# Block products in the two feed-forward layers of a 4-layer network: seven for eight

## The chip, the cores and the metric

The kernel is one program on one core of a Trainium2 chip, in float32. The metric is the device time of one execution in microseconds (us), lower is better. Time before: median 2104.29 us of 3 executions (2102.86 to 2108.72).

## The reference, cut to what matters

The network has 256 tokens of width 1024. Two layers with a mixture of 32 experts come first; then two layers of another block, each a mixer and a gated feed-forward. The change is in the feed-forwards (and in the order in which the weights of the second mixer, `mixer_c`, are loaded):

```python
def rmsnorm_2(x, g):
    xf = x.astype(jnp.float32)
    return xf * lax.rsqrt(jnp.mean(xf * xf, axis=-1, keepdims=True) + EPS) * g

def swiglu(x, w1, w3, w2):
    return (jax.nn.silu(x @ w1) * (x @ w3)) @ w2
...
        x = x + rmsnorm_2(mix, norm_g[layer, 1])
        h = rmsnorm_2(x, norm_g[layer, 2])
        x = x + rmsnorm_2(swiglu(h, ffn_w1[layer], ffn_w3[layer], ffn_w2[layer]), norm_g[layer, 3])
```

Here h is 256 x 1024, w1 and w3 are 1024 x 2816, w2 is 2816 x 1024.

## The kernel before, in words

**Stages.** The program is a list of stages. In each, TensorE (PE), VectorE (DVE), ScalarE (ACT) and GpSimd have their own instruction list; every engine waits at a stage's end until all four are through (`run_stages`, L235). SyncE (SP) runs beside them and only issues the loads of weights, in one fixed order.

**The ring.** Weights go through a ring of 6 slots of 2 MB (`WeightRing`). SP issues unit n as soon as TensorE has released the unit that held the slot before (L250, L251). A release is a drain of TensorE with an increment of `weights_used`.

**Feed-forward, up.** `feed_forward` (L1909) cuts the 2816 columns of w1 and w3 into chunks of 512 (the last one 256). A unit is one chunk of w1 or of w3. For each tile f of 128 columns (22 of them, `FT`) TensorE makes 8 matmuls with w1 and 8 with w3 (L1937): the weights' 128 x 128 block is the stationary operand, hT (h transposed: 128 channels x 256 tokens) the moving one. Both results lie in one PSUM bank. ScalarE takes the silu of the first half (L1972), VectorE multiplies it with the second half into aT (L1978). TensorE waits for a bank only from the ninth tile on. The first two tiles' products with tokens 0 to 127 are made earlier, by `up_ahead` (L1895), while the norm of tokens 128 to 255 is still being computed; `c_ahead` (L1904) does the same for the mixer behind the first feed-forward.

**Feed-forward, down.** A unit is 4 row tiles of w2 (the last one 2), 6 units in all. For each row tile and each half of the tokens TensorE makes two matmuls (L1945), with aT's 128 x 128 block as stationary and 512 columns of w2 as moving operand, into 4 banks. The last two units go first over tokens 0 to 127, then over 128 to 255, so that the first half's result is ready early.

**The norm behind it.** `residual_norm` handles the result by halves of the tokens, t = 0 and t = 1: ScalarE squares it out of PSUM (L1797), VectorE and ScalarE make the root, VectorE scales (L1824) and adds to x (L1827). Unless it is the last layer, a second norm follows on x (L1805 to L1834), TensorE turns the result (L1849), ScalarE and VectorE bring it to hT (L1811, L1838). TensorE's order: turns of t = 0, the work ahead, turns of t = 1.

**A float32 matmul in the trace** is two records of MATMUL and two of LDWEIGHTS. So L1937 has 704 matmuls and 1408 records.

Of the kernel before, what the change touches and what calls it, by code (L numbers as in the profile page):

```python
# [13 lines left out]
ALU = mybir.AluOpType  # L14
ACT = mybir.ActivationFunctionType
# [5 lines left out]
P = 128  # L21
D = 1024
S = 256
TT = S // P
KD = D // P
# [124 lines left out]
def columns(w, c0, n):  # L150

    return w[:, c0:c0 + n].rearrange("(k p) n -> p k n", p=P)


def build_program(nc, A, out):

    with ExitStack() as ctx:
# [3 lines left out]
        def sem(name):  # L161
            return ctx.enter_context(nc.semaphore(name))
# [59 lines left out]
        chain = {}  # L222
# [17 lines left out]
        def release(pe):  # L240

            pe.drain().then_inc(weights_used, 1)
# [1523 lines left out]

        def residual_norm(ready, n, scale_cols, ahead=None):

# [13 lines left out]
            halves = [slice(512 * half, 512 * half + 512) for half in range(2)]  # L1782
            each = 1 if scale_cols is None else 2

            def at(t):
# [8 lines left out]
            def act_tile(act, t):  # L1794
                act.wait_ge(ready, base + 2 * t + 2)
                for half in range(2):
                    ins = act.activation(xn[:, t, halves[half]], ps[:, 2 * half + t, :], ACT.Square,  # L1797
                                         accum_out=ssq[:, 2 * half + t:2 * half + t + 1])
# [14 lines left out]
            def dve_tile(dve, t):  # L1813
# [9 lines left out]
                for half in range(2):  # L1823
                    ins = dve.scalar_tensor_tensor(out=xn[:, t, halves[half]], in0=ps[:, 2 * half + t, :], scalar=r,  # L1824
                                                   in1=row_gain[:, halves[half]], op0=ALU.mult, op1=ALU.mult)
                v(ins)
                dve.tensor_tensor(x[:, t, :], x[:, t, :], xn[:, t, :], ALU.add).then_inc(x_ready, 1)  # L1827
                if scale_cols is None:
                    return
# [4 lines left out]
                dve.tensor_scalar(xn[:, t, :], x[:, t, :], r, None, ALU.mult).then_inc(scaled, 1)  # L1834
                for k in (0, 1, 4, 5):
# [46 lines left out]
        block_ready = sem("block_ready")  # L1882
        ffn_signals = [sem(f"ffn_{n}") for n in ("up_ready", "silu_done", "act_ready")]

# [22 lines left out]
        def feed_forward(layer, scale_cols, ahead=None):  # L1907
# [5 lines left out]
            for c, n in chunks:  # L1913
                ring.add(("w1", c), columns(w1, c, n), KD, n)
                ring.add(("w3", c), columns(w3, c, n), KD, n)
            for r, n in rows:
                ring.add(("w2", r), w2[r * P:(r + n) * P, :].rearrange("(k p) n -> p k n", p=P), n, D)
# [3 lines left out]
            silu = take(2, S)  # L1921
            up_ready, silu_done, act_ready = ffn_signals
            pe_tile, act_after, dve_after = residual_norm(block_ready, 2 * layer + 1, scale_cols, ahead)
            f0 = FT * layer

            def pe_(pe):
                f = 0
                for c, n in chunks:
                    a = ring.take(pe, ("w1", c))
                    b = ring.take(pe, ("w3", c))  # L1930
                    for j in range(n // P):
                        if f >= 8:
                            pe.wait_ge(act_ready, f0 + f - 7)
                        s0 = P if f < F_AHEAD else 0
                        for i, w in enumerate((a, b)):
                            for k in range(KD):
                                ins = pe.matmul(ps[:, NEXT_BANKS[f % 8], i * S + s0:(i + 1) * S], w[:, k, j * P:(j + 1) * P],  # L1937
                                                hT[:, k, s0:S], start=(k == 0), stop=(k == KD - 1))
                        ins.then_inc(up_ready, 1)
                        f += 1  # L1940
                    pe.drain().then_inc(weights_used, 2)
                pe.wait_ge(act_ready, f0 + FT)
                def down(w, r, k, t):
                    for half in range(2):
                        ins = pe.matmul(ps[:, 2 * half + t, :], aT[:, r + k, t * P:(t + 1) * P],  # L1945
                                        w[:, k, 512 * half:512 * half + 512], start=(r + k == 0), stop=(r + k == FT - 1))
                        if r + k == FT - 1:
                            ins.then_inc(block_ready, 1)

                for r, n in rows[:-2]:  # L1950
                    w = ring.take(pe, ("w2", r))
                    for k in range(n):
                        for t in range(TT):
                            down(w, r, k, t)
                    release(pe)
                units = [(r, n, ring.take(pe, ("w2", r))) for r, n in rows[-2:]]
                for t in range(TT):
                    for r, n, w in units:
                        for k in range(n):
                            down(w, r, k, t)  # L1960
                        if t == TT - 1:
                            release(pe)
                for t in range(TT):
                    pe_tile(pe, t)

            def act_(act):
                load_gain(act, 2 * layer + 1, A["norm_g_2"][layer, 3])
                for f in range(FT):
                    act.wait_ge(up_ready, f0 + f + 1)
                    if f >= 2:  # L1970
                        act.wait_ge(act_ready, f0 + f - 1)
                    act.activation(silu[:, f % 2, :], ps[:, NEXT_BANKS[f % 8], 0:S], ACT.Silu).then_inc(silu_done, 1)  # L1972
                act_after(act)

            def dve_(dve):
                for f in range(FT):
                    dve.wait_ge(silu_done, f0 + f + 1)
                    dve.tensor_tensor(aT[:, f, :], silu[:, f % 2, :], ps[:, NEXT_BANKS[f % 8], S:2 * S], ALU.mult).then_inc(act_ready, 1)  # L1978
                dve_after(dve)
# [479 lines left out]
        def mixer_c():  # L2459
            n0 = len(ring.units)  # L2460
            UNIT_ORDER = (2, 3, 0, 1, 4, 5, 6, 7)
            for c in UNIT_ORDER:
                ring.add(("c_in", c), columns(A["c_w_in_2"][0], 512 * c, 512), KD, 512)
            for c in range(2):
                ring.add(("c_out", c), columns(A["c_w_out_2"][0], 512 * c, 512), KD, 512)
            stream.append(stream_units(n0, len(ring.units)))
            take = carve(0, 17 * 1024)
# [395 lines left out]
```

## Time and profile before

| what | before |
|---|---|
| median time of 3 executions | 2104.29 us |
| span of the profiled execution | 2101.5 us |
| TensorE busy in the span | 1719.3 us (82%) |
| VectorE / ScalarE busy in the span | 492.5 / 233.1 us |
| feed-forward 0: up, down, norm and work ahead | 1447.9 to 1596.9, to 1674.7, to 1686.2 us |
| feed-forward 1: up, down with the final norm | 1867.0 to 2015.9, to 2101.5 us |

Of the profiled execution only the span is given; the median over the executions is 2.8 us above it. Read the table from the bottom: the two feed-forwards are 472.8 us of the span, in which the load of weights is far from its limit and TensorE is at work nearly all the time.

### The profile page before, as it was taken

How to read it: one execution, taken by the hardware profiler on the slowest of the kernel's cores; microseconds unless marked ns; L12 is line 12 of the kernel's file. 1: busy time of each engine (PE TensorE's matmuls, PEld its weight loads, DVE VectorE, ACT ScalarE, POOL GpSimd, SP SyncE). 2: the span in 40 equal slices, each digit the busy share in tenths (PEclk: the TensorE clock that was granted, in tenths of full speed). 3: DMA queues.
4: the chain of work that ended last, by engine and by line, in shares of the span. 5: the costliest groups of instructions: out<-in, count | busy, mean ns of one | idle time of the engine just before them, and what ended most of it. 6: DMA issues, size and time to landing. Idle time of an engine off the chain costs nothing.

```text
span 2101.5 us, 23283 instructions
## 1 busy us (share of the span) xinstructions
PE 1719.3 (82%) x9372; PEld 998.6 (48%) x9373; DVE 492.5 (23%) x1197; ACT 233.1 (11%) x574; POOL 92.8 (4%) x125
## 2 busy tenths in 40 slices
PE   5999978866575578776766658989999999999998
PEld 3654544322222154332222215767885486678853
DVE  1213452110111126411101104962000113320001
ACT  1002121000000011000000002322000122220000
POOL 1001001000000000840000000000000000000000
PEclk9999999987878789998787879999999999999999
DMA  9969259999999994999999996215435444124330
GB/s 361 406 249 375 111 216 396 421 421 422 422 422 422 398 405 167 413 406 421 422 422 422 422 416 250 80 64 188 159 121 194 169 148 159 42 99 151 120 140 20
DMA packets 122668, 581.16 MB, mean 277 GB/s; under 512 B 10820, under 2 KB 15272, under 8 KB 67160
## 3 DMA queue, kind: packets, MB, share of 16 engines
q1 hardware_dynamic: 120416, 573.92, 68.2%
q10 hardware_dynamic: 1064, 3.17, 0.5%
q0 software_dynamic: 1104, 2.86, 0.4%
q8 instruction: 63, 1.03, 0.2%
q14 instruction: 21, 0.17, 0.0%
HBM read 578.88 MB, written 1.05 MB: 276 GB/s over the span
## 4 chain that ended last, share of the span: by engine, by line
PE 56%; DMA 30%; DVE 6%; issue 3%; SPq 2%; ACT 1%; DVEq 1%; PEldq 0%; PEld 0%; ACTq 0%
DMA ring_buffer<-in_exp_w 29%; PE ps L1937 14%; PE ps L1945 7%; PE ps L1355 7%; PE ps L1380 4%; PE ps L2507 4%; PE ps L748 3%; PE ps L1872 3%; PE ps L506 2%; PE ps L761 1%; PE ps L910 1%; PE ps L2498 1%; SPq L1249 1%; DMA ring_buffer<-in_ada_w 1%; PE ps L859 1%
## 5 line engine op out<-in xcount | busy, mean ns | idle before, releaser
L1355 PE MATMUL ps<-ring_buffer,arena 128*32 128x512 f32 x2048 | 304.5, 752 | 183.2 <-DMA ring_buffer<-in_exp_w 180.6
L1937 PE MATMUL ps<-hT,ring_buffer 128*128 128x256 f32 (+1 forms) x1408 | 293.5, 370 | 5.2 <-issue 2.7
L1937 PEld LDWEIGHTS ps<-hT,ring_buffer 128*128 128x128 f32 x1408 | 256.5, 190 | 41.8 <-issue 6.4
L1355 PEld LDWEIGHTS ps<-ring_buffer,arena 128*32 128x32 f32 x2048 | 81.1, 134 | 393.4 <-issue 333.9
L1380 PE MATMUL ps<-ring_buffer,arena 128*32 128x512 f32 x1088 | 152.9, 714 | 93.1 <-DMA ring_buffer<-in_exp_w 82.1
L1945 PE MATMUL ps<-ring_buffer,arena 128*128 128x512 f32 x352 | 154.2, 595 | 3.0 <-DVE arena L1978 1.9
L1380 PEld LDWEIGHTS ps<-ring_buffer,arena 128*32 128x32 f32 x1088 | 40.7, 129 | 194.1 <-issue 181.4
L1551 DVE TENSOR_TENSOR arena<-arena,ps 128x512 f32<-128x512 f32 x18 | 19.1, 1063 | 415.2 <-PE ps L1355 415.2
L1945 PEld LDWEIGHTS ps<-ring_buffer,arena 128*128 128x128 f32 x352 | 65.9, 190 | 90.4 <-issue 87.8
L1978 DVE TENSOR_TENSOR arena<-arena,ps 128x256 f32<-128x256 f32 x44 | 18.5, 421 | 279.6 <-ACT arena L1972 279.6
L1324 PEld LDWEIGHTS ps<-arena,xn 128*128 128x128 f32 x640 | 73.3, 192 | 14.0 <-issue 13.9
L2507 PE MATMUL ps<-hT,ring_buffer 128*128 128x256 f32 (+1 forms) x384 | 77.7, 363 | 2.4 <-DVEq L238 1.3
L1324 PE MATMUL ps<-arena,xn 128*128 128x128 f32 x640 | 76.1, 277 | 0.7 <-DVE arena L1521 0.7
L2507 PEld LDWEIGHTS ps<-hT,ring_buffer 128*128 128x128 f32 x384 | 67.6, 190 | 12.8 <-issue 3.3
L1472 ACT ACTIVATE arena<-ps,mod,gain 128x128 f32<-128x128 f32 x72 | 27.1, 457 | 389.5 <-PE ps L1324 389.5
L748 PE MATMUL ps<-hT,ring_buffer 128*128 128x256 f32 x256 | 57.8, 387 | 4.1 <-ACTq L238 3.4
L1396 PE MATMUL ps<-arena 128*128 128x512 f32 x128 | 59.3, 605 | 0.0
L1569 DVE TENSOR_TENSOR arena<-ps,gates 128x512 f32<-128x512 f32 x16 | 11.1, 692 | 201.4 <-PE ps L1380 201.4
L1872 PE MATMUL ps<-ring_buffer,hT 128*128 128x512 f32 x128 | 56.0, 595 | 1.0 <-DVEq L238 0.8
L1489 ACT ACTIVATE arena<-ps 128x512 f32<-128x512 f32 x18 | 10.8, 597 | 409.8 <-PE ps L1355 409.8
L506 PE MATMUL ps<-ring_buffer,arena 128*32 128x512 f32 x384 | 49.6, 636 | 8.0 <-DMA ring_buffer<-in_ada_w 7.2
L748 PEld LDWEIGHTS ps<-hT,ring_buffer 128*128 128x128 f32 x256 | 49.4, 194 | 13.7 <-ACTq L238 3.5
(512 smaller groups left out, 1629.4 us busy)
## 6 DMA issues: line engine op xcount, KB each, us to landing
ring_buffer<-in_exp_w SPq DMA_DIRECT2D x384, 1024.0 KB, 18.6
ring_buffer<-in_ffn_w SPq DMA_DIRECT2D x30, 2048.0 KB, 9.1
ring_buffer<-in_ada_w SPq DMA_DIRECT2D x24, 2048.0 KB, 12.6
ring_buffer<-in_c_w_in SPq DMA_DIRECT2D x8, 2048.0 KB, 9.0
ring_buffer<-in_attn_w_in SPq DMA_DIRECT2D x6, 2048.0 KB, 17.1
ring_buffer<-in_ab_w_in SPq DMA_DIRECT2D x3, 2048.0 KB, 20.3
ring_buffer<-in_ffn_w SPq DMA_DIRECT2D x6, 1024.0 KB, 9.2
ring_buffer<-in_attn_w_o SPq DMA_DIRECT2D x2, 2048.0 KB, 12.9
```

What stands on the lines that cost most here:

```text
L506: pe.matmul(ps[g * WIDE:(g + 1) * WIDE, COND, :], spread_c[:, 2 * pair + k, row:row + WIDE], w[:, k, 512 * n:512 * (n + 1)], start=(first ...
L748: ins = pe.matmul(ps[:, n % BANKS, 0:S], w[:, k, j * P:(j + 1) * P], hT[:, k, :], start=(k == 0), stop=(k == KD - 1))
L761: ins = pe.matmul(ps[:, n % BANKS, :], hT[:, k, t * P:(t + 1) * P], w[:, k, :], start=(k == 0), stop=(k == KD - 1))
L1324: ins = pe.matmul(ps[:, BXA + k // 4, (k % 4) * P:(k % 4 + 1) * P], xn[:, t, k * P:(k + 1) * P], pick[:, t, :], start=(t == 0), stop=(t == ...
L1355: ins = pe.matmul(ps[c, bank, :], tokens[:, 4 * phase + k, c], halves[j][:, k, :], start=(phase == 0 and k == 0), stop=(phase == 1 and k = ...
L1380: ins = pe.matmul(ps[c, bank, :], tokens[:, 2 * phase + k, c], halves[j][:, k, half * 512:(half + 1) * 512], start=(phase == 0 and k == 0) ...
L1396: ins = pe.matmul(ps[:, 2 * half + t, :], weights[:, t, :], values[:, half * 512:(half + 1) * 512], start=opens, stop=False, skip_group_ch ...
L1472: return eng.activation(o, src, ACT.Identity, scale=G[:, k:k + 1], bias=H[:, k:k + 1])
L1872: ins = pe.matmul(ps[:, 2 * c + t, :], fT[:, k, t * P:(t + 1) * P], w[:, k, :], start=(k == 0), stop=(k == KD - 1))
L1937: ins = pe.matmul(ps[:, NEXT_BANKS[f % 8], i * S + s0:(i + 1) * S], w[:, k, j * P:(j + 1) * P], hT[:, k, s0:S], start=(k == 0), stop=(k == ...
L1945: ins = pe.matmul(ps[:, 2 * half + t, :], aT[:, r + k, t * P:(t + 1) * P], w[:, k, 512 * half:512 * half + 512], start=(r + k == 0), stop= ...
L2507: ins = pe.matmul(ps[:, NEXT_BANKS[n % 8], s0:S], w[:, k, j * P:(j + 1) * P], hT[:, k, s0:S], start=(k == 0), stop=(k == KD - 1))
```

## The change

In the feed-forwards most matrix products are made on 2 x 2 blocks by seven block products with sums before and after, in place of eight (Winograd's form of Strassen's method).

- **Up.** The first chunk (tiles 0 to 3, `PLAIN`) is as before. The other 18 tiles go as N = 9 pairs: a pair is two column tiles of w1 and of w3, cut in two over channels (4 + 4 tiles of 128) and over the columns; h is cut over channels and tokens. Each of the seven products is 2 x 4 matmuls (w1 and w3, four channel tiles) with 128 moving columns. VectorE makes the sums of h once (`sum_h`), three sums of the weights for each pair and one in place (`sum_w`), and joins the products (`join`). ScalarE copies four partial sums out of PSUM for each pair (`keep`) and takes one silu of 512; VectorE multiplies (`gate`).
- **Down.** The rows of w2 in a unit are cut in two, the columns in 512 + 512, the tokens in 128 + 128. VectorE sums aT (`sum_a`) and w2 (`sum_w2`); each product has half as many matmuls as the unit has row tiles, with 512 moving columns, and its own PSUM bank. The last three units go product by product. VectorE then adds the products (`dve_` and `rest_of_second`, which runs inside `dve_tile` of t = 0, behind its last scaling). The norm reads SBUF (`mixed`) where it read PSUM.
- **Ring.** The feed-forwards use slots 0 to 3; the sums lie in slots 4 and 5 (`piece`) and in spare parts of the arena. The loads of `mixer_c` get written-out slots, and all but the first wait for the end of the first feed-forward's stage.

The core of the diff:

```diff
+            UP_ORDER = (P5, P1, P2, P3, P6, P4, P7)
+            DOWN_ORDER = (P1, P2, P6, P5, P3, P7, P4)
+            LAST = 3
...
+                    pe.wait_ge(sums_done, summed("w", g))
+                    if g >= 2:
+                        pe.wait_ge(sums_done, summed("joined", g - 2))
+                    elif g == 1:
+                        pe.wait_ge(act_ready, a0 + PLAIN)
+                    for product in UP_ORDER:
+                        if product in (P3, P6, P7):
+                            pe.wait_ge(kept, kept0 + 4 * g + (P3, P6, P7).index(product) + 1)
+                        name, opens, stationary, moving = operands[product]
+                        o = region(g, name)
+                        for m in range(2):
+                            for k in range(4):
+                                ins = pe.matmul(o[:, m * P:(m + 1) * P], stationary(m, k), moving[:, k, :],
+                                                start=(opens and m == k == 0), stop=(k == 3), skip_group_check=True)
+                        ins.then_inc(part_ready, 1)
...
+                for v in range(len(rows) - LAST):
+                    w = ring.take(pe, ("w2", rows[v][0]))
+                    pe.wait_ge(sums_done, summed("a", v))
+                    pe.wait_ge(sums_done, summed("w2", v))
+                    for product in DOWN_ORDER:
+                        if v == 0 and product in (P1, P5):
+                            pe.wait_ge(sums_done, summed("joined", N - 2 + (P1, P5).index(product)))
+                        down(v, w, product)
                     release(pe)
...
+                    v(dve.tensor_tensor(s3, w11, w21, ALU.subtract))
+                    v(dve.tensor_tensor(w21, w21, w22, ALU.add))
+                    v(dve.tensor_tensor(s2, w21, w11, ALU.subtract))
+                    dve.tensor_tensor(s4, w12, s2, ALU.subtract).then_inc(sums_done, 1)
...
+                sum_h()
+                sum_w(0)
+                for f in range(2):
+                    gate_plain(f)
+                sum_w(1)
+                for f in range(2, PLAIN):
+                    gate_plain(f)
+                dve.wait_ge(act_ready, a0 + PLAIN)
+                sum_a(0)
+                for g in range(N):
+                    join(g)
+                    if g + 2 < N:
+                        sum_w(g + 2)
+                    if g == N - 2:
+                        sum_w2(0)
+                    gate(g)
+                    if g % 2 or g == N - 1:
+                        sum_a(1 + g // 2)
+                for i in range(1, len(rows)):
+                    sum_w2(i)
...
+            def rest_of_second(dve):
+                v = chain["dve"]
+                dve.wait_ge(part_ready, down_part(P7))
+                v(dve.tensor_tensor(first_sum, first_sum, ps[:, DOWN_BANK[P7], :], ALU.add))
+                dve.tensor_tensor(mixed(1, 1), second_sum, ps[:, DOWN_BANK[P7], :], ALU.add).then_inc(block_ready, 1)
+                dve.wait_ge(part_ready, down_part(P4))
+                dve.tensor_tensor(mixed(1, 0), first_sum, ps[:, DOWN_BANK[P4], :], ALU.add).then_inc(block_ready, 1)
...
-            for c in UNIT_ORDER:
-                ring.add(("c_in", c), columns(A["c_w_in_2"][0], 512 * c, 512), KD, 512)
+            for c, slot in zip(UNIT_ORDER, (2, 4, 5, 3, 0, 1, 2, 3)):
+                ring.add(("c_in", c), columns(A["c_w_in_2"][0], 512 * c, 512), KD, 512, slot=slot)
...
+            stream.append(stream_units(n0, n0 + 1))
+            stream.append(lambda sp: sp.wait_ge(stage_done, sums_used))
+            stream.append(stream_units(n0 + 1, len(ring.units)))
```

## Rows read from the trace of the kernel before

**Rows 1.** The page: granted TensorE clock in 40 slices of the span (tenths)

```profile
PEclk9999999987878789998787879999999999999999
```

**Rows 2.** Busy time by stretch: us, PE, PEld, DVE, ACT, POOL, PEclk, DMA share, GB/s

```profile
1447.90:1596.90 149.00, 146.74 (x704) 128.26 (x704) 9.27 (x22) 9.72 (x23) 0.00 (x0) 1.00 0.37 131
1596.90:1674.70 77.80, 77.10 (x177) 32.96 (x177) 4.18 (x9) 4.10 (x9) 0.00 (x0) 1.00 0.44 160
...
2015.90:2101.50 85.60, 77.09 (x176) 32.94 (x176) 6.23 (x12) 4.22 (x11) 0.00 (x0) 0.97 0.13 49
```

**Rows 3.** Timeline of feed-forward 0, up: start us, us, engine, line, operation, records

```profile
1455.38 0.38 ACT L1972 ACTIVATE arena<-ps 128x256 f32<-128x256 f32 x1 [3.19 <-PE ps L1937]
1462.29 0.38 ACT L1972 ACTIVATE arena<-ps 128x256 f32<-128x256 f32 x1 [6.53 <-PE ps L1937]
...
1525.67 27.87 PE L1937 MATMUL ps<-hT,ring_buffer 128*128 128x256 f32 x128 [0.26 <-issue]
1553.80 27.87 PE L1937 MATMUL ps<-hT,ring_buffer 128*128 128x256 f32 x128 [0.26 <-issue]
```

**Rows 4.** The same view, tiles of 128 moving columns (work ahead, mixer behind)

```profile
1438.31 7.22 PEld L1895 LDWEIGHTS ps<-hT,ring_buffer 128*128 128x128 f32 x64 [1.03 <-ACT hT L1811]
1438.31 7.41 PE L1895 MATMUL ps<-hT,ring_buffer 128*128 128x128 f32 x64 [0.79 <-ACT hT L1811]
...
1690.07 0.38 ACT L2524 ACTIVATE arena<-ps 128x256 f32<-128x256 f32 x1 [0.24 <-PE ps L2507]
1691.86 0.38 ACT L2524 ACTIVATE arena<-ps 128x256 f32<-128x256 f32 x1 [1.40 <-PE ps L2507]
```

**Rows 5.** The page's group of weight loads for L1937: busy us, mean ns

```profile
L1937 PEld LDWEIGHTS ps<-hT,ring_buffer 128*128 128x128 f32 x1408 | 256.5, 190 | 41.8 <-issue 6.4
```

**Rows 6.** The chain in order of time, feed-forward 0: start us, us, what

```profile
1596.93 14.00 PE ps L1945 x32
...
1611.02 13.99 PE ps L1945 x32
...
1674.69 0.67 PE ps L1849 x4
...
1676.57 7.41 PE ps L1904 x64
1683.98 0.96 PE ps L1849 x8
```

**Rows 7.** Groups by form, VectorE and ScalarE: busy us, mean ns, idle before

```profile
L1978 DVE TENSOR_TENSOR arena<-arena,ps 128x256 f32<-128x256 f32 x44 | 18.5, 421 | 279.6 <-ACT arena L1972 279.6
L2274 DVE TENSOR_TENSOR ring_buffer<-ring_buffer,xn 128x1024 f32<-128x1024 f32 x4 | 4.9, 1224 | 0.1
L2395 DVE TENSOR_TENSOR ring_buffer<-consts 128x512 f32<-128x512 f32 x3 | 1.9, 686 | 0.0
L2690 ACT COPY arena<-ps 128x256 f32<-128x256 f32 x8 | 3.0, 372 | 15.7 <-PE ps L2624 15.7
L1797 ACT ACTIVATE xn<-ps 128x512 f32<-128x512 f32 x16 | 9.4, 602 | 174.6 <-PE ps L1945 143.0 <-PE ps L1872 31.6
```

**Rows 8.** Timeline of attention's heads: TensorE, groups of 128 columns between waits

```profile
206.20 0.38 PE L862 MATMUL ps<-consts 128*128 128x128 f32 x2
206.43 0.60 PE L873 MATMUL ps<-consts,arena 128*128 128x128 f32 x4
206.96 0.44 PE L885 MATMUL ps<-arena 128*64 128x128 f32 x4
```

**Rows 9.** DMA issues at 1408.2 and at 1581.5: KB, us to landing

```profile
ring_buffer<-in_ffn_w SPq DMA_DIRECT2D x1, 2048.0 KB, 7.9
...
ring_buffer<-in_ffn_w SPq DMA_DIRECT2D x1, 2048.0 KB, 8.8
```

**Rows 10.** Timeline of the norm behind feed-forward 0's down

```profile
1663.98 0.60 ACT L1797 ACTIVATE xn<-ps 128x512 f32<-128x512 f32 x1 [67.55 <-PE ps L1945]
1671.50 0.75 DVE L1834 TENSOR_SCALAR xn<-x,small 128x1024 f32<-128x1024 f32 x1
```

More of the change, by code:

```diff
@@ L1828, in dve_tile @@
                 if scale_cols is None:
+                    if t == 0 and between is not None:
+                        between(dve)
                     return
@@ new lines, in feed_forward @@
+            aS = take(3, FT // 2, P)
+            hS = take(4, 4, P)
+            joint = take(2, 2, 4, P)
+            silu = take(2, 4 * P)
+            spare = take(2, 1024)
+            keep = xn.rearrange("p t d -> p (t d)").rearrange("p (b n c) -> p b n c", b=2, n=4)
+            piece = [ring_buffer[:, 4 + n // 4, (n % 4) * 1024:(n % 4 + 1) * 1024] for n in range(8)]
+            piece += [spare[:, 0], spare[:, 1]]
+            piece += [hS.rearrange("p a k c -> p (a k c)")[:, n * 1024:(n + 1) * 1024] for n in range(2)]
@@ new lines, in feed_forward @@
+            piece += [joint[:, n].rearrange("p m q c -> p (m q c)") for n in range(2)]
+            piece += [silu.rearrange("p b n -> p (b n)")]
+            silu_done, act_ready, sums_done, part_ready, kept = ffn_signals
+            PLAIN = 4
+            fast = [(c, n, j) for c, n in chunks[1:] for j in range(n // 256)]
+            N = len(fast)
+            SETS = ((1, 3, 4, 5), (0, 2, 6, 7))
+            a0 = (PLAIN + N) * layer
+            part0, kept0 = (PLAIN + 7 * N + 7) * layer, (4 * N + 1) * layer
@@ new lines, in feed_forward, with summed, region, both @@
+            for g in range(N):
+                SUMS += [("joined", g)] + [("w", g + 2)] * (g + 2 < N) + [("w2", 0)] * (g == N - 2) + [("a", 1 + g // 2)] * (g % 2 or g == N - 1)
+            SUMS += [("w2", i) for i in range(1, len(rows))]
+            def summed(*what):
+                return len(SUMS) * layer + SUMS.index(what if len(what) > 1 else what[0]) + 1
+            def region(g, name):
+                return ps[:, SETS[g % 2]["XYZW".index(name)], 0:S]
+            def both(c, n):
+                i = n0 + 2 * (c // 512)
+                slot = ring.slots[i]
+                return ring_buffer[:, slot:slot + 2, 0:KD * n].rearrange("p m (k n) -> p m k n", k=KD)
@@ new lines, in act_ @@
+                for g in range(N):
+                    for i, (product, name) in enumerate(((P5, "Y"), (P1, "X"), (P6, "X"), (P7, "X"))):
+                        act.wait_ge(part_ready, part(g, product))
+                        act.copy(keep[:, g % 2, i, :], region(g, name)).then_inc(kept, 1)
+                    act.wait_ge(sums_done, summed("joined", g))
+                    act.wait_ge(act_ready, a0 + PLAIN + g - 1)
+                    act.activation(silu[:, g % 2, :], joint[:, g % 2, 0].rearrange("p q c -> p (q c)"), ACT.Silu).then_inc(silu_done, 1)
@@ new lines, in sum_w2 @@
+                def sum_w2(i):
+                    r, n = rows[i]
+                    half = n // 2
+                    unit = n0 + 2 * len(chunks) + i
+                    dve.wait_ge(weights_landed[ring.slots[unit]], ring.landed_at[unit])
+                    if i == 1:
+                        dve.wait_ge(part_ready, part(N - 2, P7))
+                    if i == 2:
+                        dve.wait_ge(part_ready, part(N - 1, P7))
+                    if i == 5:
+                        dve.wait_ge(weights_used, n0 + 2 * len(chunks) + 1)
+                    w = ring.view(unit, n, D)
+                    w11, w12, w21, w22 = w[:, 0:half, 0:512], w[:, 0:half, 512:1024], w[:, half:n, 0:512], w[:, half:n, 512:1024]
+                    d1, d2, d4 = d_parts(i)
+                    v(dve.tensor_tensor(d1, w12, w11, ALU.subtract))
+                    v(dve.tensor_tensor(d2, w22, d1, ALU.subtract))
+                    v(dve.tensor_tensor(w12, w22, w12, ALU.subtract))
+                    dve.tensor_tensor(d4, w21, d2, ALU.subtract).then_inc(sums_done, 1)
```

217 lines of the change are left out of this document (164 added, 53 removed).

## The prediction

> **What bounds the kernel now.** I read the page's clock row first, then the busy time by stretch, the timelines of TensorE, the chain in order of time, and the groups of VectorE and ScalarE. The clock row falls only in the experts' part; in both feed-forwards TensorE has its upper level, 2.4 GHz [rows 1]. In feed-forward 0 TensorE is busy 146.7 of 149.0 us in the up part and 77.1 of 77.8 us in the down part, with the DMA engines at 0.37 and 0.44 and VectorE and ScalarE under 10 us each; the second one's down part has the same 77.1 us [rows 2]. So TensorE's stream sets these 450 us. Saving products pays only if a product keeps its price when it is made smaller, and if VectorE's sums stay hidden. The rest of the kernel is untouched but for the start of the second mixer.
>
> **The price of a matmul record.** A tile of L1937 is 32 records, and the silus of two tiles start 6.91 us apart: 215.9 ns for 256 columns [rows 3]. For 128 columns, a tile of 16 records takes 1.79 us, 111.6 ns each; the work ahead confirms it, 64 records in 7.41 us, of which 0.27 us is the last one's tail [rows 4]. So half the columns cost 51.7% of the time. That is close to the edge: there the weight loads are busy 7.22 of 7.41 us [rows 4]. For 512 columns 32 records take 14.00 us with the tail, 429 ns each [rows 6].
>
> The Trainium skill ("TensorE: Matmul & The Clock Gate", section "The mechanism") says that a weight load overlaps matmuls in flight only when its row group differs. Every product here uses all rows, so by that rule load and stream would add up. The trace disagrees: loads are shown at 190 ns each [rows 5], yet the records follow each other every 111.6 ns. A form of it is the first rival below.
>
> **The sum, part by part.**
>
> 1. *Up, products.* Before, a pair of tiles is 64 records at 215.9 ns, 13.82 us. After, it is 7 x 8 matmuls, 112 records at 111.6 ns, 12.50 us. Saved: 1.32 us, 11.9 us for the 9 pairs of a layer, 23.8 us in all. The first four tiles stay.
>
> 2. *Down, products.* Before, 22 x 4 matmuls are 176 records; after, 7 x 11 are 154. The 22 fewer, at 429 ns, are 9.4 us. Three releases stand in the stream where five stood, at 0.36 us (14.09 us from one unit to the next, less 32 records) [rows 6]: 0.7 us. For two layers 20.2 us.
>
> 3. *Waits of TensorE that are already met.* The pair adds about four points at which TensorE passes waits (its start, P3, P6, P7), 72 in both layers. In the up part such waits before 256-column tiles cost nothing: 128 records with four of them take 27.87 us, as 128 x 215.9 ns and the tail do [rows 3]. Between groups of 128 columns the trace has both: two records of L862 are followed after 0.23 us by L873, no gap, and four records of L873 after 0.53 us by L885, behind two waits, where 0.45 us is the stream [rows 8]. So 0 to 0.09 us; I take the middle, 0.05: 3.6 us (0 to 6.5).
>
> 4. *VectorE and ScalarE under a pair.* VectorE has operations on 256, 512 and 1024 elements at 0.42, 0.69 and 1.22 us [rows 7]. A pair costs it four joins (1.7), the sums of the weights (4 x 1.22, 4.9), the product with silu (0.7) and in every second pair the sums of aT (1.7): at most 9.1 of 12.5 us. The last two joins wait for P7 and its copy; after them the next sums are done some 6.6 us into the following pair and are needed at 12.5. ScalarE's four copies at 0.37 and a silu of 512 (0.6) are 2.1 us; each copy ends some 0.6 us after its product, while the product that overwrites the bank starts at least 1.8 us after it. Cost: nothing; the cover is TensorE's own stream, and without it a pair would take up to 9 us more. The new chunk is free of risk too: 4 MB are issued when the older chunk is released, the first 2 MB land 8.8 us later and the next some 5 us behind [rows 9], 14 us; VectorE comes to them after 14.5 us, TensorE after 25.
>
> 5. *From up to down.* This is the narrow place. w2's first unit goes to a slot released at the end of the eighth pair, T. It lands at T+8.8; VectorE, which stands before it with gate and join queued behind, sums until about T+14.0. TensorE ends its ninth pair near T+13.0 and so waits 1.1 us, where it waited 0.9 us before the first down matmul. Then P1, P2, P6 take 5.1 us, and P5 wants the last join: gate 0.7, sums of aT 1.8, join 1.7, ready at T+18.3 against T+19.2. The next unit's sums are ready near T+26.0 against T+26.5. So late by nothing, with 0.5 to 1 us of slack; I take 0.4 us a layer, 0.8 in all (0 to 6 if each link is a few tenths longer).
>
> 6. *Start of the second mixer.* Its first unit still comes early. The second is issued only at the stage's end E and lands 7.9 to 8.8 us later, by the first of a burst of four [rows 9] and the first of a pair. TensorE has 4 half tiles at 1.79 us and a drain, 7.6 us. Late by 0.3 to 1.3 us; I take 1.0. Behind it a unit lands every 5 to 6 us and is used for 13.8.
>
> 7. *Tail of feed-forward 0.* Before, the down part ends at L = 1674.6, t = 0 is turned at once, the work ahead starts at L+2.0 and the second turns follow it directly at L+9.3, since t = 1 is scaled by then [rows 6]. After: t = 0's last product P3 ends 10 matmuls, 8.6 us, ahead of L; one add (0.7) and its latency, then the chain from square to scaled x, 8.3 us as before [rows 10], gives L+0.5. Only then VectorE makes its three adds of t = 1 (2.1 us), and behind them stand its four moves to hT (1.1 us). So the work ahead starts at L+3.9 in place of L+2.0: 1.9 us. t = 1's own chain is late by under 1 us and stays hidden under it.
>
> 8. *Tail of the last feed-forward.* Nothing is behind it. The last product needs one more add of 512 before ScalarE's square can start: 0.75 us. The first half is long through by then, as its chain ends 2 us before L.
>
> 9. *Free edits.* The sums of h (4 x 0.69 us) and the first two sets of weight sums lie under the 21 us of the four plain tiles. Four slots are enough by point 4. Reading `mixed` from SBUF in place of PSUM keeps the squares near 0.60 us [rows 7].
>
> Saved 23.8 + 20.2 = 44.0 us; given back 3.6 + 0.8 + 1.0 + 1.9 + 0.75, about 8.1. Net 36 us. The profiled span of 2101.5 becomes 2065.5; the median lies 2.8 us over the span, so 2068.
>
> **Rivals.**
>
> *A. The weight load becomes the bound (slower).* At 128 columns load and stream are level [rows 4]. The 18 pairs have 2016 such records in long rows, with stationary operands from several places. If a record took the load's shown 190 ns [rows 5], this would add 2016 x 78 ns, 158 us: 2226 us. It decides from 36/2016 = 18 ns per record on, 129.5 ns. For it: 56 loads where 32 were. Against it: 64 records in a row, and the mixer's tiles, hold 111.6 ns. 3%.
>
> *B. A wait that is met costs as much as a release.* TensorE's gap behind a drain is 0.26 us [rows 3]. 72 x 0.26 is 18.7 us in place of 3.6: 2083 us. Against it: 0.09 us at most between small groups [rows 8]. 8%.
>
> *C. VectorE comes late at the passage.* If its strided operands make an operation 20% longer, the 17 us from the landing of w2's first unit to the second unit's sums grow by 3.4, slack 0.5: some 3 us at each passage, 2074 us. Pairs would still fit (10.9 of 12.5). For it: nothing in the trace has just these shapes. Against it: VectorE's durations here follow the element count [rows 7]. 14%.
>
> *D. The products go, the time doesn't.* VectorE or the loads would have to take 12.5 us for a pair: 37% more than counted. Then 18 pairs at 13.8 us give back all of the up part, 2092 us. 2%. With it goes a granted clock that falls for part of the feed-forward, 1%: 1.2 GHz over a twelfth of them would take all the gain.
>
> *My forecast*, 2062 to 2073: 72%.
>
> **How the numbers follow.** The lower end is the forecast with the waits at nothing and half of the passages' and mixer's cost gone, 2063, less 2 us of spread: 2060. The upper takes points 3, 5 and 6 at their bounds (2068 + 2.9 + 5.2 + 0.3) and covers C: 2079 with spread. B, A and D stay outside, with what is left of the forecast's own edges. About 0.3%, 6 us, is what a measurement of this kernel tells from no change; faster than 2098 are the forecast, B, C and D, less a share of unknown mishaps; slower are A and the clock: 0.94, 0.02, 0.04.
>
> **What the profile after would show.** The matmul group of the pairs: 2016 records of 128 columns, 12.5 to 12.9 us from one pair's first copy of ScalarE to the next; a record over 120 ns speaks for A, visible gaps between products for B. The down part near 67 us before the norm. VectorE busy some 200 us more over the kernel (per layer 9 pairs at 8.3 us on average, 27 for w2, 5 for h and the tail, less 22 products of 0.42). TensorE's idle time before the first down product near 1 us, released by VectorE's sums of w2; several us there, or before P5, is C. At the second mixer's second unit a wait of about 1 us for the DMA. The work ahead of feed-forward 0 starting near 3.9 us after its last product. What would make me wrong most easily: a wait between products that I hold for met.

## The result, and the profile after

| | before | after |
|---|---|---|
| median time | 2104.93 us of 4 (2102.86 to 2108.72) | 2072.54 us of 4 (2071.45 to 2076.56) |
| span of the profiled execution | 2101.5 us | 2069.6 us |
| feed-forward 0, start to end of the stage | 238.27 us | 219.15 us |
| second mixer (`mixer_c`) | 180.74 us | 185.46 us |
| feed-forward 1, start to the end of the span | 234.56 us | 213.74 us |

The ratio of the times is 0.9851, with a 95% interval of 0.9835 to 0.9867. The forecast was 2068 us, the range 2060 to 2079: the time lies inside it, 4.5 us above the forecast. From the start of feed-forward 0 to the end the trace is 35.2 us shorter, where the prediction had counted 36. The span is only 31.9 us shorter, because feed-forward 0 starts 3.3 us later, at 1451.25 us where it was 1447.93. The change touches nothing ahead of that point. In the 12 profiled kernels that have the change or part of it, feed-forward 0 starts between 1444.5 and 1453.3 us, so 3.3 us there tell nothing.

First the page of the changed kernel: span, instructions, busy time of each engine, granted clock in 40 slices, and the three costliest groups of the new products.

```profile
span 2069.6 us, 25312 instructions
PE 1681.4 (81%) x10192; PEld 999.5 (48%) x10193; DVE 682.3 (33%) x1441; ACT 258.4 (12%) x630; POOL 93.2 (5%) x125
PEclk9999998987878789898887878999999999999999
L2050 PE MATMUL ps<-arena,ring_buffer 128*128 128x128 f32 x1152 | 133.9, 276 | 3.7 <-issue 3.7
L2079 PE MATMUL ps<-ring_buffer,arena 128*128 128x512 f32 x252 | 111.0, 594 | 3.4 <-issue 2.3
L2050 PE MATMUL ps<-hT,ring_buffer 128*128 128x128 f32 x864 | 99.4, 275 | 0.0
```

The two groups of L2050 are the 2016 records of the pairs. Their mean of 276 ns is how long one record is shown, and they overlap. The price is the distance between them, which the timeline gives. VectorE went from 492.5 to 682.3 us, 190 more (forecast: some 200), and the clock row still falls only in the experts' part. Next the busy time by stretch (the columns are those of [rows 2]): up and down part of feed-forward 0, its norm, then up and down part of feed-forward 1.

```profile
1451.20:1589.20 138.00, 134.97 (x1136) 132.16 (x1136) 76.40 (x104) 20.85 (x49) 0.00 (x0) 1.00 0.40 142
1589.20:1657.30 68.10, 67.04 (x154) 28.93 (x154) 33.77 (x47) 5.39 (x11) 0.00 (x0) 1.00 0.37 139
1657.30:1670.40 13.10, 9.38 (x80) 8.90 (x80) 8.78 (x21) 5.17 (x16) 0.00 (x0) 1.00 0.01 1
...
1855.80:1993.00 137.20, 134.97 (x1136) 132.17 (x1137) 76.67 (x104) 20.79 (x49) 0.00 (x0) 1.00 0.40 143
1993.00:2069.60 76.60, 67.04 (x154) 28.92 (x154) 37.85 (x52) 5.64 (x14) 0.00 (x0) 0.97 0.29 110
```

Beside [rows 2] the up part is 149.0 us before and 138.0 after, the down part 77.8 and 68.1. TensorE is idle only 3.0 us of the up part, and VectorE, at 76.4 us, is busy 55% of it. TensorE is still the bound. Its timeline shows the seams (start us, us, what; in brackets the idle time before it and what ended it):

```profile
1498.49 2.02 PE L2050 MATMUL ps<-arena,ring_buffer 128*128 128x128 f32 x16 [0.40 <-issue]
1500.35 5.52 PE L2050 MATMUL ps<-hT,ring_buffer 128*128 128x128 f32 x48
1505.71 7.31 PE L2050 MATMUL ps<-arena,ring_buffer 128*128 128x128 f32 x64
1512.86 5.52 PE L2050 MATMUL ps<-hT,ring_buffer 128*128 128x128 f32 x48
1518.21 5.52 PE L2050 MATMUL ps<-arena,ring_buffer 128*128 128x128 f32 x48
1524.10 2.02 PE L2050 MATMUL ps<-arena,ring_buffer 128*128 128x128 f32 x16 [0.36 <-issue]
...
1589.24 10.54 PE L2079 MATMUL ps<-ring_buffer,arena 128*128 128x512 f32 x24 [1.16 <-DVE arena L2204]
...
1601.76 12.25 PE L2079 MATMUL ps<-ring_buffer,arena 128*128 128x512 f32 x28 [0.26 <-issue]
1614.25 12.26 PE L2079 MATMUL ps<-ring_buffer,arena 128*128 128x512 f32 x28 [0.23 <-issue]
...
1657.90 1.09 PE L1856 MATMUL ps<-consts,xn 128*128 128x128 f32 x8 [0.65 <-DVE xn L1839]
1660.85 7.41 PE L1912 MATMUL ps<-hT,ring_buffer 128*128 128x128 f32 x64 [1.86 <-DVE hT L1845]
...
1670.40 7.41 PE L2766 MATMUL ps<-hT,ring_buffer 128*128 128x128 f32 x64 [1.27 <-DVEq L238]
1681.34 8.90 PE L2766 MATMUL ps<-hT,ring_buffer 128*128 128x256 f32 x40 [3.53 <-DMA ring_buffer<-in_c_w_in]
```

Read it in the order of the prediction. The 48 records from 1500.35 on are followed 5.36 us later by the next product: 111.6 ns each, as in [rows 4]. No idle time stands between products of a pair. Two pairs with the release behind them repeat after 25.61 us. Less the release of some 0.5 us, a pair takes about 12.55. Then the passage to the down part costs a wait of 1.16 us, the tail 0.65 and 1.86 us, and the second mixer 3.53 us, the largest wait that the change made. In the chain of the same kernel (the steps that followed one another without slack) that load is (start us, us, what):

```profile
1670.38 10.92 DMA ring_buffer<-in_c_w_in
```

It was issued at the stage's end, 1670.38, and took 10.92 us to land. The nearest rows [rows 9] had 7.9 and 8.8.

### The profile page after: what moved, and what is told of

It is laid out like the page before. It is cut to its first block and busy times, and to the rows that moved or that the text cites. A ratio compares the mean times of both kernels' runs of the same rounds, so it can differ in the third digit from the quotient of the medians.

```text
span 2069.6 us, 25312 instructions
## 1 busy us (share of the span) xinstructions
PE 1681.4 (81%) x10192; PEld 999.5 (48%) x10193; DVE 682.3 (33%) x1441; ACT 258.4 (12%) x630; POOL 93.2 (5%) x125
## 3 DMA queue, kind: packets, MB, share of 16 engines
HBM read 578.88 MB, written 1.05 MB: 280 GB/s over the span
## 5 line engine op out<-in xcount | busy, mean ns | idle before, releaser
L2050 PE MATMUL ps<-arena,ring_buffer 128*128 128x128 f32 x1152 | 133.9, 276 | 3.7 <-issue 3.7
L2050 PEld LDWEIGHTS ps<-arena,ring_buffer 128*128 128x128 f32 x1152 | 130.8, 192 | 5.7 <-issue 5.7
L2079 PE MATMUL ps<-ring_buffer,arena 128*128 128x512 f32 x252 | 111.0, 594 | 3.4 <-issue 2.3
L2050 PE MATMUL ps<-hT,ring_buffer 128*128 128x128 f32 x864 | 99.4, 275 | 0.0
L2050 PEld LDWEIGHTS ps<-hT,ring_buffer 128*128 128x128 f32 x864 | 97.9, 192 | 0.0
L2766 PE MATMUL ps<-hT,ring_buffer 128*128 128x256 f32 (+1 forms) x384 | 77.7, 363 | 5.8 <-DMA ring_buffer<-in_c_w_in 3.5
L2079 PEld LDWEIGHTS ps<-ring_buffer,arena 128*128 128x128 f32 x252 | 47.2, 190 | 65.0 <-issue 65.0
L2766 PEld LDWEIGHTS ps<-hT,ring_buffer 128*128 128x128 f32 x384 | 67.6, 190 | 16.2 <-DMA ring_buffer<-in_c_w_in 3.7
## 6 DMA issues: line engine op xcount, KB each, us to landing
ring_buffer<-in_ada_w SPq DMA_DIRECT2D x24, 2048.0 KB, 13.4
```

The lines of the kernel that those rows point to most:

```text
L2050: ins = pe.matmul(o[:, m * P:(m + 1) * P], stationary(m, k), moving[:, k, :], start=(opens and m == k == 0), stop=(k == 3), skip_group_che ...
L2079: ins = pe.matmul(ps[:, DOWN_BANK[product], :], tokens, values, start=(v == 0 and j == 0), stop=last)
L2766: ins = pe.matmul(ps[:, NEXT_BANKS[n % 8], s0:S], w[:, k, j * P:(j + 1) * P], hT[:, k, s0:S], start=(k == 0), stop=(k == KD - 1))
```

## The experiments

The kernels were run in three groups, each on one chip with the kernel before: `up_only`, `cin_slots`, `gain_late` and `early_adds` beside 2102.83 us; `more_waits`, `sums_plus2`, `sums_plus4` and `half_p7` beside 2106.04; `early_start`, `all_three` and a repeat of the changed kernel beside 2105.51 (median of 9). The first nine were run once each, so they are judged by the stretches of their traces and not by their times: the start of feed-forward 0 alone scatters by several us.

### up_only: only the up part uses the seven products

```diff
-                for v in range(len(rows) - LAST):
-                    w = ring.take(pe, ("w2", rows[v][0]))
...
+                pe.wait_ge(sums_done, summed("joined", N - 1))
+                pe.wait_ge(act_ready, a0 + PLAIN + N)
...
+                for r, n in rows[:-2]:
+                    w = ring.take(pe, ("w2", r))
+                    for k in range(n):
+                        for t in range(TT):
+                            down(w, r, k, t)
```

> The up products stay seven for eight; the down part is the old one (eight products, no sums of aT or w2, the norm reads PSUM). My theory (TensorE's stream alone sets both parts): feed-forward 0's stage, 219.2 us in the changed kernel, becomes 219.2 + 9.4 (22 records of 429 ns) - 1.6 (its tail) - 0.2 (passage) = about 226.8 us, and the up part stays at 25.6 us for two pairs. Rival (the down part's seven products hide a loss by VectorE's sums, and the up pairs are slowed by the sums of aT): two pairs take under 25.4 us and the stage is under 225 us.

Measured: 2092.2 us, and feed-forward 0 took 228.79 us, between 238.27 before and 219.15 after, 2.0 more than I had expected. So the up part is worth 9.5 us there and the down part 9.6, where their products alone were counted at 11.9 and 9.4. Of the up part's missing 2.4 us, 1.8 stand in front of the first down product, in the timeline of TensorE:

```profile
1588.78 56.20 PE L2065 MATMUL ps<-ring_buffer,arena 128*128 128x512 f32 x128 [2.76 <-DVE arena L2148]
```

The last pair's copy, join, silu and gate now stand before the first down product. TensorE waits 2.76 us for them, three times the old 0.93. With the down part changed as well, P1, P2 and P6 run ahead of the last join, and most of this is covered. The two parts help each other.

### half_p7: half the matmuls of P7 left out

```diff
-                            for k in range(4):
+                            for k in range(2 if product == P7 else 4):
```

> P7 is made over two of its four channel tiles: 4 matmuls fewer for a pair, 72 in all (that part of the computation is left out). Theory 1 (TensorE's stream is the bound and a record costs 111.6 ns where it stands): a pair's period falls by 8 x 111.6 ns = 0.89 us to 11.66, both feed-forwards together 16.1 us less. Theory 2 (the pair is bound by the chain of copies, joins and sums around P7): under half of this.

```profile
1496.81 2.02 PE L2050 MATMUL ps<-arena,ring_buffer 128*128 128x128 f32 x16 [0.36 <-issue]
...
1520.63 2.02 PE L2050 MATMUL ps<-arena,ring_buffer 128*128 128x128 f32 x16 [0.36 <-issue]
```

Measured: two pairs in 23.82 us in place of 25.61, so 0.895 us a pair for 8 records, 111.9 ns each. The feed-forwards took 212.29 and 206.65 us, 6.9 and 7.1 less, 13.9 together where 16.1 was expected. In the first one the work ahead lost 1.35 us to the clock (last section). In the second one the wait at the passage grew from 0.36 to 1.27 us: w2's first unit is issued one pair ahead of the passage, and a shorter pair hides that much less of its landing and its sums. So TensorE's records set the pair: taking records away shortens it at their full price, and VectorE's sums do not step in within the pairs. They do at the passage, where the last pair's gain was lost again.

### sums_plus2 and sums_plus4: more work for VectorE in every pair

One sum of the weights is made 2 more times, or 4 more times in `sums_plus4`.

```diff
+                    for _ in range(2):
+                        v(dve.tensor_tensor(s3, w11, w21, ALU.subtract))
                     v(dve.tensor_tensor(s3, w11, w21, ALU.subtract))
```

> VectorE makes the first difference of each pair's weight sums twice more (2 x 1.25 us for a pair, same result). It is then busy 7.7 to 9.1 + 2.5 = 10.2 to 11.6 us of a pair's 12.55. Theory 1 (VectorE is hidden under TensorE's stream as long as it fits): the pair's period stays at 12.55 us, the feed-forwards stay within 0.5 us of 219.2 and 213.7 us. Theory 2 (the chain of joins and sums has no slack, so that each microsecond of VectorE shows): 18 x 2.5 = 45 us more.

> The same difference four times more: 5.0 us for a pair, VectorE busy 12.7 to 14.1 us, 13.4 on average, against TensorE's 12.55. Theory 1: now VectorE sets the pace in those pairs that have a weight sum to make: some 0.9 us for a pair, less what the slack of the first pairs covers, 5 to 8 us for a layer, 10 to 16 in all. Theory 2 (some buffer lets the average be exceeded, or the waits are elsewhere): under 3 us in all.

Busy time over two pairs, first of the changed kernel, then of `sums_plus4`:

```profile
1498.49:1524.10 25.61, 25.25 (x224) 25.08 (x225) 15.73 (x22) 4.10 (x11) 0.00 (x0) 1.00 0.45 165
```

```profile
1497.97:1523.58 25.61, 25.25 (x224) 25.08 (x225) 24.96 (x31) 4.12 (x11) 0.00 (x0) 1.00 0.46 165
```

Measured: with two more sums a pair nothing moved (219.16 and 213.83 us). With four more VectorE is busy 24.96 of 25.61 us, and the pairs still take 25.61. Feed-forward 1 took 213.93 us, and feed-forward 0 221.03, of which 1.63 are the clock's in the work ahead and 0.34 a longer wait at the passage. I had expected this run to cost 10 us or more, and that was wrong. The last weight sum of three pairs in a row, in VectorE's timeline:

```profile
1533.35 1.23 DVE L2149 TENSOR_TENSOR ring_buffer<-ring_buffer 128x1024 f32<-128x1024 f32 x1
1547.07 1.23 DVE L2149 TENSOR_TENSOR ring_buffer<-ring_buffer 128x1024 f32<-128x1024 f32 x1
1559.08 1.23 DVE L2149 TENSOR_TENSOR ring_buffer<-ring_buffer 128x1024 f32<-128x1024 f32 x1
```

VectorE's round over two pairs is 25.73 us, 12.9 a pair where I had counted 13.4, and TensorE's round is 25.61 with the release, which I had left out. VectorE is only 0.12 us too slow over two pairs. The price shows elsewhere: in the changed kernel the third pair's sums are ready 6.5 us before TensorE starts that pair, here 1.2 us before, and for the last pair 0.8 us. So VectorE has slack of nearly 5 us in every pair, and four sums of 1.25 us use it up. This run stands at the edge; a fifth sum was not tried.

### more_waits: three more met waits before each product

```diff
                     for product in UP_ORDER:
+                        for _ in range(3):
+                            pe.wait_ge(sums_done, summed("w", g))
```

> Before each of the seven products of a pair TensorE passes three more waits that are met already: 21 more for a pair, 378 in all. A pair's period in the changed kernel is 12.55 us (two pairs and a release in 25.62 us), where 112 records of 111.6 ns are 12.50: so the four points of waiting cost about 0.05 us together. Theory 1 (a met wait costs next to nothing, since the loads and matmuls queued behind it catch up): under 0.2 us more for a pair, under 4 us in all. Theory 2 (the rival of the prediction, a price for each wait that was merely small in number): 0.05 us or more each, 1 us or more for a pair, 19 us or more in all.

```profile
1497.07 2.02 PE L2052 MATMUL ps<-arena,ring_buffer 128*128 128x128 f32 x16 [0.47 <-issue]
...
1522.79 2.02 PE L2052 MATMUL ps<-arena,ring_buffer 128*128 128x128 f32 x16 [0.47 <-issue]
```

Measured: two pairs took 25.72 us, 0.11 more for 42 waits, and all of it lies in the gap behind the release (0.47 for 0.36 us). Between products there is still no idle time. Behind a product of 16 records a met wait cost nothing. Where TensorE had just been drained, the three that stand there cost 0.11 us together. The feed-forwards took 218.89 and 214.99 us; of the 1.25 us more in the second, 0.6 are a longer wait at the passage (0.96 for 0.36 us) and some 0.5 the five gaps.

### cin_slots: the second mixer's first four units are issued before the stage's end

```diff
-            for c, slot in zip(UNIT_ORDER, (2, 4, 5, 3, 0, 1, 2, 3)):
+            for c, slot in zip(UNIT_ORDER, (2, 3, 0, 1, 4, 5, 2, 3)):
...
-            stream.append(stream_units(n0, n0 + 1))
+            stream.append(stream_units(n0, n0 + 4))
```

The first four go to slots that the feed-forward's own units leave; only the slots with the sums wait for the stage.

> Only the second mixer's loads change: units 1 to 3 go to slots 3, 0 and 1, which the down part frees, and are issued before the stage's end; only the units for slots 4 and 5 wait for it. My theory: the 3.5 us that TensorE waits for the second unit in the changed kernel vanish (0 to 0.1 us), everything else stays: 3.5 us less span between the first feed-forward's end and the second's start. Rival (a later unit takes the stall over, since the fifth unit now waits): a wait of 1 us or more at a later unit.

```profile
1670.82 21.59 PE L2766 MATMUL ps<-hT,ring_buffer 128*128 128x128 f32 x128 [1.26 <-DVEq L238]
```

Measured: 2067.4 us. TensorE goes through the 128 records without a stop, as before the change, and the mixer takes 180.75 us, against 180.74 before and 185.46 after. Of these 4.7 us the late load's wait is 3.3: 3.53 us, less the 0.26 that the release would cost anyway. Another 1.3 us are a lowered clock in the mixer's heads, more than 130 us behind that wait, where TensorE had been idle for 1.03 us (the changed kernel's timeline and busy time; the granted clock is the 0.50):

```profile
1812.06 0.44 PE L2924 MATMUL ps<-consts,xn 128*128 128x128 f32 x2 [1.03 <-ACT xn L2974]
```

```profile
1813.00:1816.00 3.00, 2.57 (x8) 1.71 (x7) 0.82 (x2) 0.28 (x1) 0.00 (x0) 0.50 0.00 0
```

The same idle time of 1.03 us stands here in `cin_slots`, and in `early_adds`, which keeps the late load and waits 3.79 us for it; in neither does the clock fall there, and the mixer of `early_adds` takes 184.49 us. So that the late load has a part in these 1.3 us is not shown.

### gain_late: another queue's load moved out of the way

`load_gain(act, 2, ...)` in the mixer's list for ScalarE stands behind its first 16 evictions in place of ahead of them.

```diff
             def proj_act(act):
-                load_gain(act, 2, A["norm_g_2"][1, 1])
...
                 for n in by_act[:16]:
                     evict(n)
+                load_gain(act, 2, A["norm_g_2"][1, 1])
```

> The second mixer's load of its norm gain (512 KB, issued by ScalarE at the stage's start beside the weights) comes after its first 16 evictions. Theory 1: it took transfer time from the first unit, which then lands near 9.6 us after its issue in place of 10.9. Theory 2: the late landing comes from the burst of five units alone: 10.9 us stays. The first unit of a burst of four landed after 7.9 us in the kernel before, with no load beside it, which speaks for a part of both.

The chain of this run:

```profile
1674.11 9.69 DMA ring_buffer<-in_c_w_in
```

Measured: the unit landed after 9.69 us, and TensorE waited 2.29 us. But `more_waits` and `half_p7`, which keep the small load in its place, had a wait of 2.44 us, and the other kernels 3.30 to 3.87. One run near the lower end of a scatter that was there without the edit shows nothing. The landings of all these kernels lie between 9.69 and 11.26 us, and what sets them stays open.

### early_adds: two of the three last adds earlier on VectorE

The two adds that read P7's bank run directly after x of t = 0 is written; only the add for P4 stays behind the scaling.

```diff
                 dve.tensor_tensor(x[:, t, :], x[:, t, :], xn[:, t, :], ALU.add).then_inc(x_ready, 1)
+                if t == 0 and between is not None:
+                    between[0](dve)
...
-                    between(dve)
+                    between[1](dve)
```

> VectorE's two adds that need P7 come right after x of the first half is added, in a gap of 1.2 us where it waits for ScalarE's square; only the add of P4 stays behind the last scaling. My theory: the work ahead of feed-forward 0 starts 1.3 us earlier after the last product (3.6 us in the changed kernel, so about 2.3), the stage is 1.3 us shorter. Rival (the first half's chain is itself late by the adds, since 1.4 us don't fit in 1.2): under 1.0 us gained. In the last feed-forward nothing changes.

```profile
1655.12 1.02 PE L2083 MATMUL ps<-ring_buffer,arena 128*128 128x512 f32 x2
...
1658.69 7.41 PE L1914 MATMUL ps<-hT,ring_buffer 128*128 128x128 f32 x64 [0.80 <-ACT hT L1814]
```

Measured: the work ahead starts 2.55 us after the last down product's end (1656.14) in place of 3.60, and what ends its wait is ScalarE's move and no longer VectorE's. That is 1.05 us, where 1.3 was expected. The whole of feed-forward 0 is only 0.28 us shorter, mostly since the wait at the passage happened to be 1.75 us here and not 1.16.

### early_start: the first down products do not wait for the sums of w2

P1 and P2 read w2 as it was loaded; only from P6 on are sums of it read.

```diff
-                    pe.wait_ge(sums_done, summed("w2", v))
                     for product in DOWN_ORDER:
+                        if product == P6:
+                            pe.wait_ge(sums_done, summed("w2", v))
```

> In the down part's first three units TensorE waits for VectorE's sums of w2 only before P6; P1 and P2 read the landed weights as they are. My theory: TensorE's wait at the passage (1.16 us behind VectorE in feed-forward 0 of the changed kernel, 0.36 us in feed-forward 1, some 1.2 to 1.7 us in the other runs) goes to the release's own gap of about 0.3 us, 0.8 to 1 us less for each feed-forward. Rival (prediction, point 5: the last join is the next to be late, wanted by P5 5.1 us after the first product): the wait turns up before P5 and under 0.3 us are gained.

```profile
1584.55 10.54 PE L2079 MATMUL ps<-ring_buffer,arena 128*128 128x512 f32 x24 [0.26 <-issue]
...
1656.10 7.41 PE L1912 MATMUL ps<-hT,ring_buffer 128*128 128x128 f32 x64 [1.85 <-DVE hT L1845]
```

Measured: the wait at the passage is gone (0.26 us, what a release costs), and no later one took its place. Feed-forward 0 took 218.16 us, 1.0 less. Feed-forward 1 was expected to gain as much, but its wait had been only 0.36 us, and it stayed at 213.70.

### all_three and after_again: the three edits together, and the changed kernel once more

> The second mixer's loads through the slots freed early, the two early adds, and the late wait for the sums of w2, together. My theory: 3.5 (second mixer) + 1.0 (tail of feed-forward 0) + 1.5 (two passages) = 6 us less than the changed kernel on this chip, and up to 1.7 us more where the granted clock no longer falls behind a gap: near 2066 us where the changed kernel has 2072.5. Rival (the gains eat each other, since the next thing is late at each place): under 4 us less.

> The changed kernel once more, on the same chip as the version above, so that the two can be compared: 2069 to 2077 us, 0.983 to 0.987 of the kernel before.

| | median of 5 | ratio to before | 95% interval |
|---|---|---|---|
| changed kernel again | 2071.43 us | 0.9847 | 0.9827 to 0.9866 |
| with the three edits | 2062.11 us | 0.9806 | 0.978 to 0.9831 |

```profile
1585.70 10.54 PE L2083 MATMUL ps<-ring_buffer,arena 128*128 128x512 f32 x24 [0.26 <-issue]
...
1656.21 7.41 PE L1914 MATMUL ps<-hT,ring_buffer 128*128 128x128 f32 x64 [0.80 <-ACT hT L1814]
```

Measured: the medians differ by 9.3 us, though the two intervals overlap at their edges (0.9827 to 0.9831). From the start of feed-forward 0 on, the traces take 611.7 us with the three edits and 620.8 without, 9.1 less; the trace of the first comparison had 618.4. All three waits are gone or small. The edits alone account for about 6; the other 3 us are the lowered clock, which the repeat's trace showed twice (1.63 us in the work ahead and 1.4 behind the mixer's wait) and that of `all_three` at neither place. It is the fastest version found, 43 us under the kernel before.

## Why the prediction held, point by point

1. **Up, products: right.** 111.6 ns a record in long rows from mixed sources, the same as in the work ahead. The up parts are 11.0 and 11.8 us shorter, waits included. Rival A is dead: the load shown at 190 ns never set the pace, and `half_p7` prices 8 records at 0.895 us. By the rule that a load overlaps only for another row group (the Trainium skill, "TensorE: Matmul & The Clock Gate", section "The mechanism") load and stream would add up; the trace disagrees again. The prediction's tile of 1.79 us makes 111.9 ns a record and not the 111.6 that it wrote; over 2016 records that is 0.6 us.
2. **Down, products: right.** From the first product to the end of the last: 77.65 us before, 68.01 after in feed-forward 0, and 77.65 and 67.96 in the second. That is 19.3 us for both against 20.2; each release and the start of the last phase cost a little more than counted.
3. **Met waits: mis-sized.** I took the middle between 0 and 0.09 us, 3.6 us in all. A pair costs 12.55 us, which leaves 0.05 for its four points together and 0.9 us in all, and even that lies behind the drain: the five gaps there are 0.36 to 0.40 us where they were 0.26 to 0.29, and `more_waits` moved only them. Rival B is dead with it. The gap of 0.09 us in [rows 8], behind four records only, is not explained by these runs.
4. **VectorE and ScalarE hidden: right.** VectorE is busy 15.73 us of 25.61, 7.9 a pair, with nearly 5 us of slack that `sums_plus4` uses up without a loss. Rival D, 12.5 us a pair, falls with it. An addition of 1024 elements took 1.22 to 1.23 us with its strided operands too, so rival C's premise falls. By the formula for such additions in the Trainium skill ("VectorE: DVE Perf Modes", section "The TRN2 errata — SBUF-src ops pay a fixed extra latency per instruction"), 1024 plus 151 cycles at 0.96 GHz, the estimate is 1.224 us, and the trace agrees.
5. **Passage: right for the wait, and nothing behind it.** TensorE waited 1.16 and 0.36 us where it had waited 0.93 (forecast 1.1). In feed-forward 0 the last join was done at 1592.76 us, 1.6 us before P5. The second unit's sums cost nothing. The 0.4 us a layer were 0.2 in one and a gain of 0.6 in the other.
6. **Start of the second mixer: the step that failed in size.** The mechanism was right, the price was not: 1.0 us was forecast, from landings of 7.9 to 8.8 us, and the landing took 10.92 us. The wait cost 3.3 us, and `cin_slots` gives it back. I held 1.3 for the end of the range; my bounds came from two landings, one of them the first of a burst of four, and here, as the first of five, it took longer. Why stays open. The lowered clock in the heads, 1.3 us more, stood in no term of the prediction.
7. **Tail of feed-forward 0: right.** The work ahead starts 3.60 us after the last product (forecast 3.9), and `early_adds` shows that the adds are the cause. From the last product to the stage's end it is 13.15 us for 11.62: 1.5 us, forecast 1.9.
8. **Last tail: right.** The square starts 0.76 us after the last product, forecast 0.75; the two rows are those of the timeline of VectorE and ScalarE.

```profile
2061.02 0.69 DVE L2008 TENSOR_TENSOR ring_buffer<-ring_buffer,ps 128x512 f32<-128x512 f32 x1 [0.73 <-PE ps L2079]
...
2061.74 0.63 ACT L1800 ACTIVATE xn<-ring_buffer 128x512 f32<-128x512 f32 x1 [5.67 <-DVE ring_buffer L2008]
```

The sum from the start of feed-forward 0: up parts -22.8, down parts -19.3, tail +1.5, mixer +4.7, last tail +0.7, together -35.2 us. Points 3 and 5 were 2.7 and 1.1 us too dear, point 6 2.3 us too cheap, and the clock's 1.3 us was not foreseen. These nearly cancel, so that the total is right by more than its parts deserve: that part of the hit is luck. What is left to the forecast lies ahead of the feed-forwards, 3.3 us in this trace, where the change does nothing and the start scatters by 9 us. The range's lower end, 2060, was 1 us under what its own terms give (2063 less 2); nothing hung on it.

## What to carry to other kernels

- A product of smaller blocks is worth its share only if the records keep their price per column. Read that price from any tile of the same width in the same kernel, as the distance between records and not as the mean that a group shows.
- When buffers are taken for something else, look at the first load that now waits for a stage's end. Putting the loads that can go early into the slots that come free early cost nothing and saved a wait of 3.3 us, more than the two other edits together.
- Let the products that read raw data go first: the waits for sums then lie under them (`early_start`, and the opposite in `up_only`).

## What the runs showed of the hardware

**The granted clock can fall for a moment behind a short gap of TensorE.** In these feed-forwards and in the mixer between them it did so at four places. The work ahead is 64 records that follow an idle time of 1.85 or 1.86 us. It took 7.41 us in 4 of the 9 kernels that have this gap, 9.04 in four and 8.76 in one. Busy time and granted clock over it (the last three columns are granted clock, DMA share and GB/s) in `cin_slots` and `gain_late`:

```profile
1659.64:1668.68 9.04, 9.04 (x66) 9.04 (x67) 4.18 (x9) 1.83 (x6) 0.00 (x0) 0.81 1.05 392
```

```profile
1662.95:1671.99 9.04, 9.04 (x66) 9.04 (x67) 4.18 (x9) 1.83 (x6) 0.00 (x0) 0.81 0.00 0
```

The DMA engines are full in the one (1.05) and idle in the other (0.00), so the traffic is not the cause. A granted clock of 0.81 is a mean of 2.4 GHz and a stretch at the lower level, 1.2 GHz. Behind the mixer's wait of 2.3 to 3.9 us the next 64 records took 14.08 us in 4 kernels and 15.47 to 17.09 in 6. In `up_only` both down parts start behind 2.76 us, and the 128 records there took 56.20 us once and 57.90 the other time. And behind the 1.03 us in the mixer's heads the clock fell in the changed kernel's first trace and in no other of the 13. Where the work ahead followed a gap of 0.80 us at most (`up_only`, `early_adds`, `all_three`), it took 7.41 each time. So a gap of 1.9 to 3.9 us in a busy stream cost 1.3 to 3 us more in 12 of 21 cases, beside its own length, and one of 1.03 us did it once. What decides whether it does is open.

**The first 2 MB of a burst have no fixed price.** At the start of the second mixer, in ten kernels that differ little, the landing took 9.69 to 11.26 us, against 7.9 and 8.8 us in [rows 9]; `gain_late` did not settle why.
